# Start addresses of weight parts, h and activations in SBUF, and a shared buffer for the gates' linear

## The chip, the cores and the metric

The kernel runs on one core of a Trainium2 chip. The metric is the time of one execution on the device in microseconds (us), as the median of several runs. PE is TensorE, PEld its weight loads, DVE VectorE, ACT ScalarE, POOL GpSimd, SP the engine that issues the DMAs. A matmul here has two operands in SBUF. The **stationary** one (128 columns) is brought into the array by a weight load (LDWEIGHTS), the **moving** one (up to 512 columns) is streamed past it. The profile writes `bank<-w_hi,h_hi` for either order of the two.

## The reference

A block of three sublayer groups for one sequence of 256 tokens and width 1024, all in fp32:

```python
for i in range(2):                               # first_block
    shift, scale, gate = split(silu(c) @ ada_w[i] + ada_b[i], 3)
    h = rms_norm(x, norm_g[i]) * (1 + scale) + shift
    y = nsa_mixer(h, ...) if i == 0 else moba_mixer(h, ...)
    x = x + gate * y
x = x + 0.5 * swiglu(rms_norm(x), gate, up, down)      # second_block, hidden width 2816
proj = rms_norm(x) @ w_in                              # MLA and FoX attention, two gated branches
x = x + (sigmoid(g_mla + b) * (y_mla @ w_mla) + sigmoid(g_fox + b) * (y_fox @ w_fox)) @ w_o
x = x + 0.5 * swiglu(rms_norm(x), gate, up, down)
```

Each mixer is a set of linears around an attention over 256 tokens. In the first one the gates are `sigmoid(h @ w_gate + gate_b)` for three branches of 16 heads.

## The kernel before, in words

Activations are held with the width on the partitions: `h_hi` and `h_lo` are `[128, 8, 256]`, eight tiles of 128 features by 256 tokens. To keep fp32 precision with the fp32r matmul format, each number is split into a rounded part and its rest, and a product is three matmuls: hi·hi, hi·lo and lo·hi. The same is done with the outputs of attention (`o_hi`, `o_lo`, which lie in `qs` in the first block and in `o2_hi`, `o2_lo` in the second), the latents (`l_hi`, `l_lo`) and the hidden activations of the two feed-forward layers (`a1_hi`, `a1_lo`, `a2_hi`, `a2_lo`, 22 tiles each).

Weights come in **units** of 1024 columns (4 KB on each partition). SP fetches them one after another into seven buffers `w_raw0..6`. ACT rounds a unit into `w_hi[i % 4]` (`rounds`, L1105), DVE takes the rest into `w_lo[i % 4]` (`rests`, L1651), and PE uses them. A buffer of a part is free when PE's last matmul of the unit four earlier is done. The order of the units is one list (`unit_list`), and each engine's program is written out in that order.

Three places issue the large matmuls:

- `linear`, tokens out (L493): the stationary operand is a 128-token piece of `h`, `o` or `a`, the moving one 512 columns of a weight part (360 in `mix_lat`). A unit holds two tiles of the width, so for each unit and each half of the tokens it issues `w_hi, w_lo, w_hi, w_lo` against the hi activations and then `w_hi` twice against the lo ones.
- `linear`, features out (L505): the stationary operand is 128 columns of a weight part, the moving one 256 tokens of `h` or `o`, in the order (hi, hi), (hi, lo), (lo, hi).
- `tile_products` (L879): as L493, one half of the tokens at a time.

```python
xs = (hi, lo)[q][:, k0 + k + kk, t * P:(t + 1) * P]
mm = e.matmul(pb[t][:, 0:n], xs, (wh, wl)[p][:, kk * n:(kk + 1) * n],   # L493: stationary xs, moving w
mm = e.matmul(o, ws[p], xs[q], ...                                      # L505: stationary w, moving xs
```

SBUF is given out by `sb` in the order of the program, each buffer behind the one before it, with the start rounded up to 32 bytes. `mix`, `ffn1`, `mix2` and `ffn2` are four regions that begin at the same address, right behind `mask_r`, and are used in turn. `gate_lin` (1 KB, the last of the region `mix`) holds the gates' linear of the first block: DVE adds the bias into it (L2031), ACT takes the tanh in place (L1357), PE transposes it. `gated` (2 KB, in front of it) holds the gated outputs of attention of the first block (L1844).

Of the kernel before, what the change touches and what calls it, by code (L numbers as in the profile page):

```python
# [7 lines left out]
F32, F32R, I32 = mybir.dt.float32, mybir.dt.float32r, mybir.dt.int32  # L8
# [3 lines left out]
P = 128  # L12
D = 1024
S = 256
TT = S // P
KT = D // P
# [4 lines left out]
FT = FFN // P  # L21
# [11 lines left out]
UNIT = 1024  # L33
Z_FIRST = 5
NRAW, NSPLIT = 7, 4
# [154 lines left out]
def program(nc, wts, cols_d, rows_d, const_d, pos_d, gate_bias_d, x_d, out_d):  # L190
# [7 lines left out]
    ctx = ExitStack()  # L198
    with ctx:
        def sb(name, shape, dt=F32, on=ctx):  # L200
            return on.enter_context(nc.sbuf_tensor(name, shape, dt))
# [3 lines left out]
        def signal(name, by=1):  # L205
            signals.append(Signal(ctx.enter_context(nc.semaphore(name)), by))
            return signals[-1]

        raw = [sb(f"w_raw{i}", [P, UNIT]) for i in range(NRAW)]
        w_hi = [sb(f"w_hi{i}", [P, UNIT], F32R) for i in range(NSPLIT)]  # L210
        w_lo = [sb(f"w_lo{i}", [P, UNIT], F32R) for i in range(NSPLIT)]
        x = sb("x", [P, TT, D])
        h_hi, h_lo = (sb(n, [P, KT, S], F32R) for n in ("h_hi", "h_lo"))
        scr = sb("scr", [P, TT, D])
        cols, rows, const = sb("cols", [P, NCOLS]), sb("rows", [P, NROWS]), sb("const", [P, NCONST])
        pos = sb("pos", [P, NANG], I32)
# [14 lines left out]
                                   ("moba_k", ROT), ("mla_qr", MR))}  # L231
        ada_acc = [sb(f"ada_acc{i}", [P, 512]) for i in range(2)]
        unit_r, minus_r, mask_r = (sb(n, [P, P], F32R) for n in ("unit_r", "minus_r", "mask_r"))

        col = lambda n: cols[:, COLS[n][0]:COLS[n][1]]
        row = lambda n: rows[:, ROWS[n][0]:ROWS[n][1]]
# [18 lines left out]
        mix = ExitStack()  # L255
# [14 lines left out]
        parts_of_o = sb("parts_of_o", [P, TT, 2, 3, HD], on=mix)  # L270
        vc = sb("vc", [P, NKV, HD], on=mix)
        gated = sb("gated", [P, 2, S], on=mix)
        gate_lin = sb("gate_lin", [P, S], on=mix)
        pc_t = zs[:, 8:8 + NKV, :]
        z_tok = zs[:, 0:8, :].rearrange("p (t k) s -> p t (k s)", t=TT)

# [3 lines left out]
        ffn_a = {1: [sb(f"a1_{n}", [P, FT, S], F32R, on=ffn1) for n in ("hi", "lo")]}  # L280
# [15 lines left out]
        rs_row = sb("rs_row", [P, S], on=mix2)  # L296
        mix2.close()
        ffn2 = ExitStack()
        ffn_a[2] = [sb(f"a2_{n}", [P, FT, S], F32R, on=ffn2) for n in ("hi", "lo")]
        ffn_v[2] = [sb(f"act2_{n}", [P, TT, S], on=ffn2) for n in range(2)]  # L300
        ffn2.close()

# [2452 lines left out]
```

## Time and profile before

| | |
|---|---|
| runs, median of 3 | 917.91 us (917.71 to 919.36) |
| the profiled execution: span, first to last instruction | 916.3 us |
| runs less that span | 1.6 us |
| PE busy | 890.5 us, 97% |
| PEld busy | 760.4 us, 83% |
| DVE, ACT, POOL busy | 566.8, 494.0, 174.1 us |
| granted clock of PE | full, in all slices |
| DMA | 163.26 MB, mean 178 GB/s |

The profile shows no more than the span for the profiled execution, so its own time is taken as that span plus the 1.6 us. PE's busy time is the union of its matmuls; neighbouring matmuls overlap in it, since one that has begun to stream is not yet finished. What a matmul costs in a dense stretch is therefore not its duration but the step from its start to the next start.

### The profile page before, as it was taken

How to read it: one execution, taken by the hardware profiler on the slowest of the kernel's cores; microseconds unless marked ns; L12 is line 12 of the kernel's file. 1: busy time of each engine (PE TensorE's matmuls, PEld its weight loads, DVE VectorE, ACT ScalarE, POOL GpSimd, SP SyncE). 2: the span in 40 equal slices, each digit the busy share in tenths (PEclk: the TensorE clock that was granted, in tenths of full speed). 3: DMA queues.
4: the chain of work that ended last, by engine and by line, in shares of the span. 5: the costliest groups of instructions: out<-in, count | busy, mean ns of one | idle time of the engine just before them, and what ended most of it. 6: DMA issues, size and time to landing. Idle time of an engine off the chain costs nothing.

```text
span 916.3 us, 12879 instructions
## 1 busy us (share of the span) xinstructions
PE 890.5 (97%) x4925; PEld 760.4 (83%) x4925; DVE 566.8 (62%) x918; ACT 494.0 (54%) x780; POOL 174.1 (19%) x189
## 2 busy tenths in 40 slices
PE   3999999999999999999999999999999999999998
PEld 3789898998688988888888888798889888888886
DVE  5884787638878477555555556595557655555442
ACT  3634765555647646444444447676654654444431
POOL 1026265554065500000000004270000010000000
PEclk9999999999999999999999999999999999999999
DMA  9956665456473555555556555553344655555650
GB/s 360 375 170 207 208 214 177 127 150 198 141 259 94 183 184 161 184 185 185 184 185 206 156 151 181 161 162 92 94 118 152 189 186 185 187 185 187 212 168 24
DMA packets 45836, 163.26 MB, mean 178 GB/s; under 512 B 5200, under 2 KB 5584, under 8 KB 45776
## 3 DMA queue, kind: packets, MB, share of 16 engines
q1 hardware_dynamic: 45776, 162.44, 55.0%
q8 instruction: 40, 0.66, 0.3%
q14 instruction: 20, 0.16, 0.0%
HBM read 161.37 MB, written 1.05 MB: 177 GB/s over the span
## 4 chain that ended last, share of the span: by engine, by line
PE 86%; DVE 5%; ACT 4%; DMA 2%; issue 2%; POOL 1%; SPq 0%; DVEq 0%; ACTq 0%; POOLq 0%
PE bank L493 60%; PE bank L505 8%; PE bank L520 4%; PE bank L668 2%; PE bank L674 1%; PE bank L879 1%; DVE w_lo L1651 1%; DVE ada_acc L1733 1%; PE bank L695 1%; PE bank L696 1%; PE bank L694 1%; DMA x<-in_x 1%; PE bank L751 1%; DMA w_raw<-in_weights 1%; PE bank L600 1%
## 5 line engine op out<-in xcount | busy, mean ns | idle before, releaser
L1105 ACT ACTIVATE w_hi<-w_raw 128x1024 fp32r<-128x1024 f32 (+2 forms) x249 | 259.1, 1047 | 172.4 <-PE bank L493 153.7
L1651 DVE TENSOR_TENSOR w_lo<-w_raw,w_hi 128x1024 fp32r<-128x1024 f32 (+2 forms) x249 | 301.7, 1228 | 79.2 <-ACT w_hi L1105 78.6
L493 PE MATMUL bank<-w_hi,h_hi 128*128 128x512 f32 (+1 forms) x592 | 234.4, 396 | 0.8 <-issue 0.5
L493 PE MATMUL bank<-w_lo,h_hi 128*128 128x512 f32 (+1 forms) x592 | 229.8, 388 | 0.0
L493 PE MATMUL bank<-w_hi,h_lo 128*128 128x512 f32 (+1 forms) x592 | 181.9, 388 | 0.5 <-DVE h_lo L1680 0.5
L493 PEld LDWEIGHTS bank<-w_hi,h_hi 128*128 128x128 f32 x592 | 111.4, 188 | 23.3 <-issue 1.9
L493 PEld LDWEIGHTS bank<-w_hi,h_lo 128*128 128x128 f32 x592 | 110.9, 188 | 24.0 <-DVE h_lo L1680 0.9
L493 PEld LDWEIGHTS bank<-w_lo,h_hi 128*128 128x128 f32 x592 | 111.5, 188 | 21.0
L2486 POOL TENSOR_TENSOR ada_acc<-ada_acc,w_raw 128x512 f32<-128x512 f32 x56 | 79.3, 1417 | 78.3 <-ACT w_raw L1109 73.1
L493 PE MATMUL bank<-w_hi,a_hi 128*128 128x512 f32 x176 | 69.9, 397 | 0.0
L493 PE MATMUL bank<-w_lo,a_hi 128*128 128x512 f32 x176 | 69.7, 396 | 0.0
L2276 DVE SCALAR_TENSOR_TENSOR act<-bank,stats,act 128x256 f32<-128x256 f32 x44 | 21.1, 483 | 67.5 <-ACT act L1521 67.5
L505 PE MATMUL bank<-h_hi,w_hi 128*128 128x256 f32 x200 | 58.7, 293 | 0.2 <-ACT tok_k L1109 0.2
L505 PE MATMUL bank<-h_lo,w_hi 128*128 128x256 f32 x200 | 56.5, 283 | 0.0
L505 PE MATMUL bank<-h_hi,w_lo 128*128 128x256 f32 x200 | 56.5, 282 | 0.0
L493 PE MATMUL bank<-w_hi,a_lo 128*128 128x512 f32 x176 | 55.1, 394 | 0.0
L493 PEld LDWEIGHTS bank<-w_hi,a_lo 128*128 128x128 f32 x176 | 33.0, 188 | 8.1
L493 PEld LDWEIGHTS bank<-w_hi,a_hi 128*128 128x128 f32 x176 | 33.0, 188 | 7.9
L493 PEld LDWEIGHTS bank<-w_lo,a_hi 128*128 128x128 f32 x176 | 33.0, 188 | 7.8
L505 PEld LDWEIGHTS bank<-h_hi,w_hi 128*128 128x128 f32 x200 | 38.2, 191 | 1.2 <-issue 0.8
L2466 POOL TENSOR_TENSOR stats<-stats 128x2 f32<-128x2 f32 x4 | 7.0, 1753 | 168.4 <-DVE stats L1664 168.4
L505 PEld LDWEIGHTS bank<-h_lo,w_hi 128*128 128x128 f32 x200 | 38.2, 191 | 0.4 <-issue 0.2
(318 smaller groups left out, 1421.6 us busy)
## 6 DMA issues: line engine op xcount, KB each, us to landing
w_raw<-in_weights SPq DMA_DIRECT2D x298, 512.0 KB, 4.1
w_raw<-in_weights SPq DMA_DIRECT2D x4, 360.0 KB, 3.4
x<-in_x SPq DMA_DIRECT2D x1, 1024.0 KB, 9.3
gate_row<-in_gate_bias SPq DMA_DIRECT2D x2, 512.0 KB, 6.5
out<-x SPq DMA_DIRECT2D x4, 256.0 KB, 3.2
w_raw<-in_weights SPq DMA_DIRECT2D x3, 256.0 KB, 3.6
const<-in_constants SPq DMA_DIRECT2D x1, 285.5 KB, 5.4
cols<-in_columns SPq DMA_DIRECT2D x1, 208.5 KB, 2.5
```

Source lines behind the costliest of these rows:

```text
L493: mm = e.matmul(pb[t][:, 0:n], xs, (wh, wl)[p][:, kk * n:(kk + 1) * n], start=(k + kk == 0 and q == 0 and p == 0), stop=(k + kk == kts - 1 ...
L505: mm = e.matmul(o, ws[p], xs[q], start=(k + kk == 0 and i == 0 and b % 2 == 0), stop=(k + kk == kts - 1 and i == 2 and (b % 2 == 1 or b == ...
L520: mm = e.transpose(bank[0:int(np.prod(src.shape[1:])), o:o + src.shape[0]], src, ident)
L600: mm = e.matmul(bank[:, j * P:j * P + NB], r[:, kk * 256 + j * P:kk * 256 + (j + 1) * P], flat[i][:, k + kk, :], start=(k + kk == 0 and j ...
L668: e.matmul(o, k[:, g, br, j * P:(j + 1) * P], qs[:, ha:hb + 1:2, j * P:S], start=m == 0, stop=False, skip_group_check=True)
L674: mm = e.matmul(o[:, a, (t - j) * P:(t - j + 1) * P], bcast(mx[:, t, h, it["mx"]:it["mx"] + 1], [P, P]), minus_r[:, :], start=False, stop= ...
L694: e.matmul(o[0], p[:, a * S:a * S + P], v[0], start=True, stop=True)
L695: e.matmul(o[1], p[:, a * S + P:(a + 1) * S], v[0], start=True, stop=False)
L1105: e.activation(w_hi[i % NSPLIT][:, 0:c], raw[v % NRAW][:, 0:c], ACT.Copy).then_inc(*rounded(v))
L1651: e.tensor_tensor(w_lo[i % NSPLIT][:, 0:c], raw[v % NRAW][:, 0:c], w_hi[i % NSPLIT][:, 0:c].bitcast(F32), ALU.subtract).then_inc(*rested(v))
L2276: e.scalar_tensor_tensor(v, pairs[(p0 + n) % 2][tt][:, S:2 * S], norm_rs[i][:, tt:tt + 1], v, ALU.mult, ALU.mult).then_inc(*act_done((f, n ...
L2486: e.tensor_tensor(acc, acc, raw[u % NRAW][:, kk * 512:(kk + 1) * 512], ALU.add).then_inc(*ada_summed((c, k)))
```

## The change

The weights' parts, `h_lo` and the activations of the second feed-forward layer get gaps in front of them, and `gate_lin` becomes the first half of `gated`. On every engine the instructions are the same and stand in the same order; only the addresses differ, and the name of the tile in the four instructions on `gate_lin`.

```diff
@@ -206,11 +206,23 @@
             signals.append(Signal(ctx.enter_context(nc.semaphore(name)), by))
             return signals[-1]
 
+        gaps = []
+
+        def gap(n, on=ctx):
+            gaps.append(sb(f"gap{len(gaps)}", [P, n], on=on) if n else None)
+
+        def staggered(name, words):
+            for i, n in enumerate(words):
+                gap(n)
+                yield sb(f"{name}{i}", [P, UNIT], F32R)
+
         raw = [sb(f"w_raw{i}", [P, UNIT]) for i in range(NRAW)]
-        w_hi = [sb(f"w_hi{i}", [P, UNIT], F32R) for i in range(NSPLIT)]
-        w_lo = [sb(f"w_lo{i}", [P, UNIT], F32R) for i in range(NSPLIT)]
+        w_hi = list(staggered("w_hi", (0, 16, 16, 8)))
+        w_lo = list(staggered("w_lo", (8, 8, 8, 32)))
         x = sb("x", [P, TT, D])
-        h_hi, h_lo = (sb(n, [P, KT, S], F32R) for n in ("h_hi", "h_lo"))
+        h_hi = sb("h_hi", [P, KT, S], F32R)
+        gap(16)
+        h_lo = sb("h_lo", [P, KT, S], F32R)
         scr = sb("scr", [P, TT, D])
         cols, rows, const = sb("cols", [P, NCOLS]), sb("rows", [P, NROWS]), sb("const", [P, NCONST])
         pos = sb("pos", [P, NANG], I32)
@@ -231,6 +243,7 @@
                                    ("moba_k", ROT), ("mla_qr", MR))}
         ada_acc = [sb(f"ada_acc{i}", [P, 512]) for i in range(2)]
         unit_r, minus_r, mask_r = (sb(n, [P, P], F32R) for n in ("unit_r", "minus_r", "mask_r"))
+        gap(8)
 
         col = lambda n: cols[:, COLS[n][0]:COLS[n][1]]
         row = lambda n: rows[:, ROWS[n][0]:ROWS[n][1]]
@@ -270,7 +283,7 @@
         parts_of_o = sb("parts_of_o", [P, TT, 2, 3, HD], on=mix)
         vc = sb("vc", [P, NKV, HD], on=mix)
         gated = sb("gated", [P, 2, S], on=mix)
-        gate_lin = sb("gate_lin", [P, S], on=mix)
+        gate_lin = gated[:, 0, :]
         pc_t = zs[:, 8:8 + NKV, :]
         z_tok = zs[:, 0:8, :].rearrange("p (t k) s -> p t (k s)", t=TT)
 
@@ -296,7 +309,10 @@
         rs_row = sb("rs_row", [P, S], on=mix2)
         mix2.close()
         ffn2 = ExitStack()
-        ffn_a[2] = [sb(f"a2_{n}", [P, FT, S], F32R, on=ffn2) for n in ("hi", "lo")]
+        gap(32, ffn2)
+        ffn_a[2] = [sb("a2_hi", [P, FT, S], F32R, on=ffn2)]
+        gap(16, ffn2)
+        ffn_a[2].append(sb("a2_lo", [P, FT, S], F32R, on=ffn2))
         ffn_v[2] = [sb(f"act2_{n}", [P, TT, S], on=ffn2) for n in range(2)]
         ffn2.close()
```

Where the buffers begin, as the remainder of the start address by 512 bytes. Every piece of them that a large matmul reads begins at the same remainder as its buffer (the 360-column ones of `mix_lat` apart, whose second half begins 1440 bytes on):

```
buffer            before   after
w_raw0..6         128      128
w_hi0..3          128      128, 192, 256, 288
w_lo0..3          128      320, 352, 384, 0
x, h_hi           128      0
h_lo, scr         128      64
mask_r, unit_r    288      224
a1_hi, a1_lo      288      256
o2_*, l_*         288      256
qs, kh, kl        416      384
a2_hi             288      384
a2_lo             288      448
gate_lin          416      384 (gated)
```

The buffers of a large matmul where an operand's own start is a multiple of 32 but not of 64 are, before: all of `a`, `o2`, `l`, `qs`; after: `w_hi3` and `w_lo1`. The last buffer of the region `mix` ends 544 bytes lower than before.

## Rows read from the trace of the kernel before

**Rows 1.** The page: busy time of each engine, share of the span, instructions.

```profile
PE 890.5 (97%) x4925; PEld 760.4 (83%) x4925; DVE 566.8 (62%) x918; ACT 494.0 (54%) x780; POOL 174.1 (19%) x189
```

**Rows 2.** The page: the clock that PE was granted, in 40 slices.

```profile
PEclk9999999999999999999999999999999999999999
```

**Rows 3.** Windows: stretch; its length; busy us (instructions) of PE, PEld, DVE, ACT, POOL; clock.

```profile
29.50:150.00 120.50, 118.55 (x762) 105.47 (x762) 91.90 (x167) 67.46 (x106) 47.90 (x59) 1.00 0.66 227
...
350.00:480.00 130.00, 130.00 (x599) 107.58 (x598) 74.43 (x87) 66.08 (x87) 1.62 (x1) 1.00 0.58 186
...
843.00:916.30 73.30, 70.16 (x304) 56.33 (x302) 32.67 (x31) 25.10 (x26) 0.00 (x0) 1.00 0.43 136
```

**Rows 4.** The chain that ended last: start us, us, what, count of instructions.

```profile
125.37 3.81 DMA w_raw<-in_weights
...
143.12 2.87 PE bank L505 x24
...
250.33 27.20 PE bank L493 x120
...
334.26 11.19 PE bank L493 x48
...
480.46 33.60 PE bank L493 x144
...
542.98 3.98 PE bank L493 x24
...
684.12 2.81 PE bank L505 x24
...
854.37 58.81 PE bank L493 x252
```

**Rows 5.** Groups by line: busy us, mean ns, idle before with releaser.

```profile
L493 PE MATMUL bank<-w_hi,h_hi 128*128 128x512 f32 (+1 forms) x592 | 234.4, 396 | 0.8 <-issue 0.5 <-DVE tok_q L1715 0.2
...
L493 PE MATMUL bank<-w_hi,a_hi 128*128 128x512 f32 x176 | 69.9, 397 | 0.0
...
L505 PE MATMUL bank<-h_hi,w_hi 128*128 128x256 f32 x200 | 58.7, 293 | 0.2 <-ACT tok_k L1109 0.2
...
L493 PE MATMUL bank<-w_hi,qs 128*128 128x512 f32 x104 | 34.8, 402 | 1.2 <-DVE w_lo L1651 0.8 <-issue 0.4
...
L493 PE MATMUL bank<-w_lo,qs 128*128 128x512 f32 x52 | 20.6, 395 | 0.0
...
L505 PE MATMUL bank<-o_hi,w_hi 128*128 128x256 f32 x64 | 18.4, 287 | 0.0
...
L879 PE MATMUL bank<-w_hi,qs 128*128 128x512 f32 x24 | 7.7, 396 | 0.0
...
L879 PE MATMUL bank<-w_lo,qs 128*128 128x512 f32 x12 | 4.7, 396 | 0.0
```

**Rows 6.** Timelines, PE and PEld, at 854.44 us: start us, us, the instruction.

```profile
854.44 0.40 PE L493 MATMUL bank<-w_lo,a_hi 128*128 128x512 f32 x1
...
854.44 0.19 PEld L493 LDWEIGHTS bank<-w_hi,a_hi 128*128 128x128 f32 x1
```

**Rows 7.** Timeline, PE, from 542.9 us: matmuls of 360 columns.

```profile
542.98 0.33 PE L493 MATMUL bank<-w_lo,h_hi 128*128 128x360 f32 x1
543.14 0.33 PE L493 MATMUL bank<-w_hi,h_hi 128*128 128x360 f32 x1
543.31 0.33 PE L493 MATMUL bank<-w_lo,h_hi 128*128 128x360 f32 x1
```

**Rows 8.** Groups by line: the engines that make the weights' parts.

```profile
L1651 DVE TENSOR_TENSOR w_lo<-w_raw,w_hi 128x1024 fp32r<-128x1024 f32 (+2 forms) x249 | 301.7, 1228 | 79.2 <-ACT w_hi L1105 78.6
L1105 ACT ACTIVATE w_hi<-w_raw 128x1024 fp32r<-128x1024 f32 (+2 forms) x249 | 259.1, 1047 | 172.4 <-PE bank L493 153.7 <-DMA w_raw<-in_weights 15.4 <-PE bank L505 3.2
```

**Rows 9.** The tile gate_lin, then gated: duration min/median/max, first and last start.

```profile
L1357 ACT ACTIVATE gate_lin<-gate_lin x1: 422/422/422, 97.6 to 97.6; 128x256 f32<-128x256 f32 x1
...
L1844 DVE SCALAR_TENSOR_TENSOR gated<-bank,zs x4: 672/680/682, 175.1 to 221.6; 128x512 f32<-128x512 f32 x4
```

## The prediction

> **What bounds the kernel now.** I read the page's busy times first. PE is busy 97% of the span, no other engine over 62% [rows 1], and its clock is granted in full throughout [rows 2], which is the 2.4 GHz level. The windows tell where PE is the only limit: from 350 to 480 us it is busy for 130.00 of 130.00 us, and from 843 us on it lacks only the output's tail [rows 3]. From 29.5 to 150 us it is busy 118.55 of 120.50 us, but there the chain of waits also runs through other engines and transfers, for instance 3.81 us on a weight fetch [rows 4]. From 250 us on the chain is nearly one row of PE after another. So what counts is the **step** from one matmul's start to the next, and the chain's rows give it: us by count.
>
> The steps, from [rows 4], for a moving operand of 512 columns, which takes 512 / 2.4 = 213.3 ns at this clock:
>
> - stationary `h`, from 250.33 us: 27.20 / 120 = 226.7 ns, 13.4 over the columns;
> - stationary `qs`, from 334.26 us: 11.19 / 48 = 233.1 ns, 19.8 over;
> - stationary `a1`, from 480.46 us: 33.60 / 144 = 233.3 ns, 20.0 over; `a2`, from 854.37 us: 58.81 / 252 = 233.4 ns.
>
> For 256 moving columns (106.7 ns) they are 2.87 / 24 = 119.6 ns with `h` moving and 2.81 / 24 = 117.1 ns with `o2` moving, 12.9 and 10.4 over. The 360 columns of `mix_lat` (150.0 ns) step by 3.98 / 24 = 165.8 ns, 15.8 over.
>
> So one shape, 128 x 128 against 512 columns, costs 226.7 or 233.3 ns, by nothing that the program says except where the stationary operand lies. The next weight load starts with the matmul: a matmul with `w_lo` and the load for its successor, with `w_hi`, both start at 854.44 us [rows 6], so two reads of SBUF run together. The weights lie at remainder 128 of 512 bytes; `h` lies there too, `a` at 288 and `qs` at 416. The engines that make the weight parts are not the limit: ACT waited 153.7 us for PE to free a buffer, DVE 78.6 us for ACT [rows 8], and PE's idle time ahead of these matmuls is 0.8 and 1.2 us [rows 5].
>
> The Trainium skill speaks against any effect here. TensorE: Matmul & The Clock Gate, Step-by-step (Part 2), says that PE has two independent SBUF read ports, so that loading the next weights takes no bandwidth from the running matmul. SBUF — State Buffer, A bandwidth-pool intuition that's wrong, says that slowdowns come from a port lock and not from shared bandwidth. By these rules `h` and `a` would step alike; the 6.6 ns between them are not explained by them.
>
> **The change, part by part.** It adds and removes no instruction and moves none, so every engine's queue and every wait stays as it is.
>
> *1. The activations leave the odd remainders.* What parts the cheap from the dear steps in these rows can be read in two ways: by the distance between the two reads (0 for `h`, 160 for `a`, 288 for `qs`), or by whether the stationary operand begins at a multiple of 64 bytes (128 does; 288 and 416 don't). I take the second for this term: distances of 160 and 288 cost the same to 0.2 ns, which a position that mattered by itself would hardly do. After the change `a1`, `a2`, `l` and `qs` all begin at multiples of 64. The matmuls against `a` are 3 x 176 = 528, against `qs` 104 + 52 + 24 + 12 = 192 [rows 5]; together 720. Each falls from 233.4 to 226.7 ns: 720 x 6.7 = **4.8 us less**. Between the ends: nothing, or down to the 10.4 ns over the columns that `o2` shows, 720 x 9.6 = 6.9 us. Nearly all lie in stretches that are PE alone, so they count in full.
>
> *2. `o2` as moving operand.* It leaves 288, where it stepped 2.5 ns faster than `h`. There are 3 x 64 = 192 such matmuls [rows 5]: **0.5 us more**, if `h`'s price becomes its own.
>
> *3. The weights and `h` spread.* With `h_hi` at 0 and `h_lo` at 64, the weight parts at eight remainders, the distance 0 between a 512-column read and the next load is left only for `w_lo3`. By the reading of part 1 this does nothing for six of eight parts. `w_hi3` and `w_lo1` begin at 288 and 352, off 64 bytes. As moving operands they have a witness: the second half of each unit of `mix_lat` begins at remainder 32, and its step is 0.17 us against 0.16 us for the one in front [rows 7], no difference at this resolution. As stationary operands at L505 they are a quarter of 3 x 200 + 3 x 64 = 792; at worst 198 x 6.7 = 1.3 us more, at best nothing. I take **0**, since the short rows show no 6.7 ns anywhere. The whole of `h` at L493, 3 x 592 = 1776 matmuls, is the large unknown: one nanosecond on each is 1.8 us. Its ends are in the rivals.
>
> *4. ACT, DVE, DMA.* Their operands move too. Rounding takes 1047 ns and the rest 1228 ns a unit, 249 units each [rows 8], 259.1 and 301.7 us of 916.3. Even 10% more on both would stay hidden behind PE, for whom ACT waits 153.7 us; if that cover went, DVE's 78.6 us of waiting would be the next to go. **0**.
>
> *5. `gate_lin` in `gated`.* ACT's tanh is at 97.6 us, and `gated` is first written at 175.1 us [rows 9]. No wait is added. **0**.
>
> Sum: −4.8 + 0.5 = **−4.3 us**. The profiled execution has a span of 916.3 us, which becomes 912.0 us; the 1.6 us between span and the runs' median (917.9 us) put the forecast at **913.6 us**.
>
> **The rivals.**
>
> *A, it is the distance, and the chosen ones are good.* The loads' and the streams' reads meet in the same part of SBUF, and the spread keeps them apart. For it: `o2` at another distance costs 10.4 ns over the columns where `h` costs 12.9; all three distances seen at 512 columns cost more than that. If all large matmuls fell to 10.4 over: `h` at L493 1776 x 3.0 = 5.3 us, the 720 others 6.9 us, `h` at L505 600 x 2.5 = 1.5 us, in all 13.7 us less, **904.2 us**. Against it: no distance in the rows is near the bare columns, and the spread gives each pair another distance, so they can't all be the best.
>
> *B, nothing happens.* The 6.6 ns come from something that goes with the stage (the order over tiles, the banks), and addresses don't matter: **917.9 us**. This is what the skill's two pages above would give. Against it: `qs` and `a` come in stages with different orders and cost the same. That the change doesn't do what it says is out: the built program has the addresses.
>
> *C, slower: distance 0 was the cheap one.* Where both reads begin in the same place, the load follows the stream through SBUF and never crosses it; at every other distance they meet. For it: at 512 columns distance 0 is the cheapest of all rows, 226.7 against 233.1 and 233.4. The change takes `h` away from 0 in all but about 70 of its 1776 matmuls. If they step as `a` does now, that is 1700 x 6.7 = 11.4 us more, and `a` gains almost nothing, so **929 us** is its end; in the middle, half of that, **923.6 us**. It decides against the forecast from 4.3 us / 1776 = 2.4 ns on each `h` matmul. Against it: the 256-column rows, where 0 (119.6) is dearer than the other distance (117.1).
>
> **How the numbers follow.** The chances: forecast 0.35, A 0.26, B 0.12, C 0.27. A measurement of this kernel can tell about 0.2%, 1.8 us, from no change. The forecast and A are faster, B is the same, C is slower; a hundredth of the forecast's share goes to no change: 0.60, 0.13, 0.27. The likeliest single time is 913.6 us, its own range by the ends of parts 1 to 3 being 911.0 (6.9 less) to 914.9 (4.8 less, 0.5 and 1.3 more). The range for all cases runs from 902.0, a little below A, to 924.0, the middle of C; what lies above that is C's far end, and what lies below 902 would need steps that no row shows.
>
> **What would show it right or wrong.** In the changed kernel's chain the last PE row, 252 matmuls against `a2`, should fall from 58.81 to 57.1 us, the row of 144 against `a1` from 33.60 to 32.6 us, and the 48 against `qs` from 11.19 to 10.9 us, while the 120 against `h` stay at 27.20. If the `h` row falls as well, towards 26.8 us, A is right. If it rises to 27.6 us or more, C is. If no row moves, B. Unequal steps for the four buffers within one stretch, with `w_hi3` and `w_lo1` apart from the rest, would show that 64 bytes matter for the moving operand too.

## The result, and the profile after

The changed kernel takes 924.29 us (median of 6 runs, 923.33 to 927.26) against 917.95 us for the kernel before in the same set: a ratio of 1.0064, 95% interval 1.0051 to 1.0077. It is **slower by 6.3 us**.

The page of the changed kernel: its span, busy times as in [rows 1], and the granted clock.

```profile
span 925.5 us, 12879 instructions
...
PE 898.5 (97%) x4925; PEld 761.6 (82%) x4925; DVE 566.6 (61%) x918; ACT 494.0 (53%) x780; POOL 172.1 (19%) x189
...
PEclk9999999999999999999999999999999999999999
```

PE's instructions are the same 4925, and the busy times of the engines that feed it have not moved (DVE 566.8 to 566.6, ACT 494.0 to 494.0); POOL fell from 174.1 to 172.1 us. PE grew by 8.0 us, its weight loads by 1.2 us. The chain that ended last, with the rows that answer to those of [rows 4] (start us, us, what, count; line 493 is now 509, line 505 is 521):

```profile
146.97 2.88 PE bank L521 x24
...
254.15 27.85 PE bank L509 x120
...
338.95 11.12 PE bank L509 x48
...
487.55 33.38 PE bank L509 x144
...
698.35 11.48 PE bank L521 x96
...
852.58 11.15 PE bank L509 x48
864.17 58.17 PE bank L509 x252
```

By step: `h` as the stationary operand 27.85 / 120 = 232.1 ns, where it was 226.7; `qs` 11.12 / 48 = 231.7 (233.1 before); `a1` 33.38 / 144 = 231.8 (233.3); `a2` 58.17 / 252 = 230.8 (233.4). The last stretch of 48 against `h` takes 11.15 us, 11.00 before. At 256 moving columns nothing much changed (2.88 / 24 = 120.0 ns, 119.6 before). So the cheap steps and the dear ones have met near 231 ns, and `h` has by far the most matmuls. An estimate from the rows: 1776 x 5.4 = 9.6 us more on `h`; less on `a` (0.22 and 0.64 us in the two rows, 396 of its 528 matmuls, so 1.1 in all) and on `qs` (192 x 1.4 = 0.3 us). That is 8.2 us. Between the medians it is 6.3 us, so the estimate is too high, and its nearness to the 8.0 us more of busy time is in part chance, since the profiled execution is a long one. The term of `h` is the one that is too large. Summed from their starts in the trace of the kernel `weights_h_spread` below, which ran at the full clock throughout, the 1488 matmuls of 512 columns against `h` behind 250 us take 348.4 us, where they took 341.7 us before, and the 288 ahead of it, where PE also waits for other engines, 0.8 us more: some 7.5 us in all. The 600 matmuls of 256 columns with `h` give 0.7 us back.

The profiled execution has 3 us that the others lack: it is the run of 927.26 us, the other five lie between 923.33 and 924.48. Early on PE waited 1.75 us for `w_lo`, whose weights had come late (ACT had waited 6.94 us for that fetch, 5.37 us in the kernel before), and behind that wait it lost its clock for a while. The timeline of PE and two windows (stretch, length, busy us of PE, clock, DMA share, GB/s) of the changed kernel:

```profile
42.74 0.47 PE L509 MATMUL bank<-w_hi,h_hi 128*128 128x512 f32 x1 [1.75 <-DVE w_lo L1667]
```

```profile
40.00:45.00 5.00, 2.80 (x11) 0.91 0.98 389
45.00:50.00 5.00, 5.00 (x18) 0.75 0.87 311
```

From 45 to 50 us the granted clock averages 0.75, so PE was at its lower level, 1.2 GHz, for half of the time; it issues 18 matmuls, where 5 us hold 22 steps of 226.7 ns. The five other executions lack the 3 us, so this is not counted as a cost of the change. They have no trace; their mean granted clocks are 0.999 and 1.0, this one's 0.998.

### The profile page after: what moved, and what is told of

Its sections match the earlier page's. It is cut to its first block, busy times and chain, and to the rows that moved or that the text cites. A ratio compares the mean times of both kernels' runs of the same rounds, so it can differ in the third digit from the quotient of the medians.

```text
span 925.5 us, 12879 instructions
## 1 busy us (share of the span) xinstructions
PE 898.5 (97%) x4925; PEld 761.6 (82%) x4925; DVE 566.6 (61%) x918; ACT 494.0 (53%) x780; POOL 172.1 (19%) x189
## 4 chain that ended last, share of the span: by engine, by line
PE 87%; DVE 4%; ACT 4%; DMA 3%; issue 1%; POOL 1%; SPq 0%; DVEq 0%; ACTq 0%; POOLq 0%
PE bank L509 60%; PE bank L521 8%; PE bank L536 4%; PE bank L684 2%; DMA w_raw<-in_weights 2%; PE bank L690 1%; PE bank L895 1%; PE bank L711 1%; PE bank L712 1%; PE bank L710 1%; DMA x<-in_x 1%; DVE w_lo L1667 1%; PE bank L767 1%; ACT w_hi L1121 1%; PE bank L616 1%
## 5 line engine op out<-in xcount | busy, mean ns | idle before, releaser
L1121 ACT ACTIVATE w_hi<-w_raw 128x1024 fp32r<-128x1024 f32 (+2 forms) x249 | 259.2, 1047 | 177.3 <-PE bank L509 157.1
L1667 DVE TENSOR_TENSOR w_lo<-w_raw,w_hi 128x1024 fp32r<-128x1024 f32 (+2 forms) x249 | 301.8, 1229 | 81.8 <-ACT w_hi L1121 81.3
L509 PE MATMUL bank<-w_hi,h_hi 128*128 128x512 f32 (+1 forms) x592 | 237.5, 401 | 2.3 <-DVE w_lo L1667 1.7
L509 PE MATMUL bank<-w_lo,h_hi 128*128 128x512 f32 (+1 forms) x592 | 232.6, 393 | 0.0
L509 PE MATMUL bank<-w_hi,h_lo 128*128 128x512 f32 (+1 forms) x592 | 185.8, 395 | 0.5 <-DVE h_lo L1696 0.5
L2277 DVE SCALAR_TENSOR_TENSOR a_lo<-bank,a_hi 128x512 fp32r<-128x512 f32 x22 | 15.2, 692 | 37.9 <-ACT a_hi L1125 37.9
```

Of the source, the lines that this page charges most:

```text
L1121: e.activation(w_hi[i % NSPLIT][:, 0:c], raw[v % NRAW][:, 0:c], ACT.Copy).then_inc(*rounded(v))
L1667: e.tensor_tensor(w_lo[i % NSPLIT][:, 0:c], raw[v % NRAW][:, 0:c], w_hi[i % NSPLIT][:, 0:c].bitcast(F32), ALU.subtract).then_inc(*rested(v))
L2277: e.scalar_tensor_tensor(a_lo[:, 2 * n:2 * n + 2, :], b[:, :].rearrange("p (k t) -> p k t", k=2), 1.0, a_hi[:, 2 * n:2 * n + 2, :].bitcast ...
```

## The experiments

"Distance" is the start of the next stationary operand less the start of the running matmul's moving operand, modulo 512 bytes. All kernels compute the whole reference. In all of them `gate_lin` is the first half of `gated`, which pays for the gaps. A step is a chain row's time by its count, so a mean; "over" is that less 512 / 2.4 = 213.3 ns, which serves as the zero of the scale: no row here comes near it.

### All operands at one remainder

```diff
+        gap(88)                      # behind mask_r: the four regions begin at 128
-        qs = sb("qs", [P, NH, S], F32R, on=mix)
+        gap(96, mix)
+        qs = sb("qs", [P, NH, S], F32R, on=mix)
```

> The kernel before, with gate_lin in gated, and one gap ahead of the four regions and one ahead of qs, so that a, o2, l and qs begin at remainder 128 like the weights and h. Theory D (the step follows the distance between the moving operand and the next stationary one, 0 is cheapest): the 252 matmuls against a2 fall from 58.81 to 57.1 us, the 144 against a1 from 33.60 to 32.6, the 48 against qs from 11.19 to 10.9, h stays at 227; 913 us. Theory S (the stage sets it, not the address): nothing moves, 918 us. Theory 64 (multiples of 64 are cheap): as D here.

Measured: **914.38 us** against 918.40 us, ratio 0.9959 (0.9946 to 0.9971). It is faster than both kernels. The chain:

```profile
333.61 10.93 PE bank L500 x48
...
479.47 32.69 PE bank L500 x144
...
689.09 11.70 PE bank L512 x96
...
840.75 10.92 PE bank L500 x48
852.10 57.19 PE bank L500 x252
```

`qs` 227.7 ns, `a1` 227.0, `a2` 226.9: each fell from 233 to about what `h` costs, in the same stages with the same order and the same banks. The address alone does it. That part of the forecast's working (6.7 ns on each of 720 matmuls) has its size right, but not its reason: this kernel cannot tell a multiple of 64 from a distance of 0. The `o2` row (96 matmuls) went from 11.46 to 11.70 us, the size that part 2 gave for `o2` at the weights' remainder.

### Only the weights and h spread

```diff
-        w_hi = [sb(f"w_hi{i}", [P, UNIT], F32R) for i in range(NSPLIT)]
-        w_lo = [sb(f"w_lo{i}", [P, UNIT], F32R) for i in range(NSPLIT)]
+        w_hi = list(staggered("w_hi", (0, 16, 16, 8)))
+        w_lo = list(staggered("w_lo", (8, 8, 8, 32)))
...
         h_hi = sb("h_hi", [P, KT, S], F32R)
+        gap(16)
         h_lo = sb("h_lo", [P, KT, S], F32R)
+        gap(16)                      # all that follows begins as before
```

> Only the gaps of the weights' parts and of h as in the change, with a gap behind h_lo so that all that follows begins at the remainders of before. Theory D: h rises as in the change, from 227 to about 232 ns a matmul, and the activations (a against the spread weights) come near 232; 924 us. If the activations' move was what cost time in the change, this stays at 918 us.

Measured: **924.01 us**, ratio 1.0063 (1.0049 to 1.0076), the change's whole loss. The chain, `h` first, then `a2`:

```profile
250.29 27.85 PE bank L506 x120
...
860.29 58.47 PE bank L506 x252
```

`h` costs 232.1 ns as in the changed kernel. `a2`, which has not moved, costs 232.0, down from 233.4 by the weights' new places alone. So the activations' own moves, which the change makes besides, change nothing measurable on top of this: 924.01 us here (1.0063), 924.29 us with them (1.0064).

### Only the activations moved

```diff
+        gap(120)                     # behind mask_r: a1, o2, l at 256, qs at 384
...
+        gap(32, ffn2)                # a2_hi at 384
+        gap(16, ffn2)                # ahead of a2_lo: 448
```

> Only the activations' start as in the change (a1 256, a2 384 and 448, o2 and l 256, qs 384), weights and h at 128 as before. Theory 64: a and qs fall to 226.7 ns, 913 us. Theory D: a1 at distance 128, a2 at 256 and 320, qs at 256, each some 230 to 233 ns, since only 0 is cheap; 916 to 918 us.

Measured: **916.84 us**, ratio 0.9984 (0.9973 to 0.9995). The chain, `qs`, `a1`, `a2`:

```profile
333.37 10.93 PE bank L502 x48
...
479.41 33.60 PE bank L502 x144
...
853.30 58.28 PE bank L502 x252
```

`a1` begins at 256, a multiple of 64 like all operands here, and still costs 233.3 ns. That fells the reading on which the forecast stood. `qs`, at a distance of 256, costs 227.7 ns, as much as at 0 in `all_at_128`. This was foreseen by no theory and led to the scans. The small gain is `qs` and a part of `a2`, 58.28 us where it was 58.81. The two halves of the change do not add up: 1.6 us less here and 5.6 us more in `weights_h_spread` make 4.0 us more, and together they measured 6.3. The intervals, about 1 us either way each, leave room for a part of that.

### h moved to the distance that a has

```diff
+        gap(40)
         h_hi = sb("h_hi", [P, KT, S], F32R)
         h_lo = sb("h_lo", [P, KT, S], F32R)
+        gap(88)
```

> The kernel before, with h_hi and h_lo moved from remainder 128 to 288 and nothing else moved (gate_lin in gated pays for the gaps). Theory D: h gets the distance 160 that a has, so its 1776 matmuls step by 233.3 instead of 226.7 ns: 11 us more, 929 us, and 120 of them take 28.0 us instead of 27.20. Theory 64: the same, since 288 is off 64 bytes. Theory S: 918 us.

Measured: **927.70 us**, ratio 1.0098 (1.0085 to 1.0112), 9.3 us more. The chain:

```profile
251.82 28.00 PE bank L501 x120
...
852.35 11.20 PE bank L501 x48
```

28.00 us for 120, to the hundredth what was expected, 233.3 ns. `h` is only a stationary operand in these matmuls, so the address of what the weight loads read sets the step, together with the address of what streams. The whole is about 2 us less than the 11: the 256-column matmuls with `h` became a little cheaper (2.81 to 2.85 us for 24, from 2.87), and ahead of 250 us other engines share the chain.

### The scan of distances

Four kernels, one run each, with gaps that put `h`, `qs`, `a1` and `a2` at four different distances at a time; in the last, slices that begin four elements into a buffer eight elements longer.

```diff
+        gap(16)                      # scan_64, ahead of h_hi; 64 in scan_256, 120 in scan_480
+        gap(80)                      # scan_64, behind mask_r; 80 in scan_256, 48 in scan_480
+        gap(16, ffn2)                # scan_64, ahead of a2; 120 in scan_256, 8 in scan_480
...
+        def shifted(name, kt, on=ctx):     # scan_16
+            return sb(name, [P, kt * S + 8], F32R, on=on)[:, 4:4 + kt * S].rearrange("p (k s) -> p k s", k=kt)
```

> Weights all at 128; the distance from the moving weights to the next stationary operand is 64 for h, 160 for qs, 32 for a1, 96 for a2. Theory D (each distance has its own price): qs near 20 ns over the 213.3 of its columns, as a and h were at 160; h, a1 and a2 give new points, each above the 13.7 of distance 0. Theory D2 (price repeats every 256 bytes, since qs cost 15.2 at 256 as well as at 0): h at 64 then like 320. Theory M (what cost time in the change was that successive operands begin at different remainders, not the distance): all of them near 14.

> Distances 256 for h, 352 for qs, 224 for a1, 192 for a2, the same within each. Theory D2: h stays at 226.7 ns a step, since 256 is like 0. If h costs 20 over its columns here, the 15.2 of qs at 256 were its own. Theory M: all near 14.

> Distances 480 for h, 448 for qs, 320 for a1, 352 for a2. Theory D2: a2 at 352 like 96, h at 480 like 224, a1 at 320 like 64. Theory M: all near 14. A step under 13 ns over the columns would show a place better than 0, and give a layout faster than both kernels.

> Distances that are no multiple of 32: 16 for h, 96 for qs, 496 for a1, 48 for a2 (slices that begin four elements into their buffers). Theory D with fine structure: 16 and 496 differ from 0 and from each other; if a collision of the two reads is what costs, a shift by one line of 16 bytes either way should change the 13.7 ns, to under 10 or over 17. If only multiples of 32 bytes count, h stays at 13.7.

A fifth followed, with slices of two, six and four elements:

> Distances of 8 for h, -8 (504) for a1, -48 (464) for a2, the same within each. By the points so far (-16: 15.0, 0: 13.7, 16: 18.9, 32: 19.9; 192: 15.6, 224: 20.0): h between 13.7 and 18.9, a1 between 13.7 and 15.0, a2 between 15.6 and 20. Below 13.7 anywhere would give a layout better than all at one remainder.

The times were 927.03, 918.88, 928.16, 925.94 and 922.70 us, beside 918.59 us for the kernel before (918.34 for the last). The chains, in this order: `h`, `qs` (in `scan_480` alone; the row is 11.19 us in `scan_64` and 11.24 us in `scan_256`), `a1`, `a2`.

```profile
251.54 28.00 PE bank L503 x120
...
485.82 33.59 PE bank L503 x144
...
863.05 59.05 PE bank L503 x252
```

```profile
251.49 27.20 PE bank L503 x120
...
481.96 33.60 PE bank L503 x144
...
856.23 57.71 PE bank L503 x252
```

```profile
252.63 28.00 PE bank L503 x120
...
337.59 11.00 PE bank L503 x48
...
486.58 33.60 PE bank L503 x144
...
864.18 59.05 PE bank L503 x252
```

```profile
253.06 28.00 PE bank L509 x120
...
486.74 32.90 PE bank L509 x144
...
862.17 58.80 PE bank L509 x252
```

```profile
250.76 27.68 PE bank L509 x120
...
483.37 33.60 PE bank L509 x144
...
859.31 58.43 PE bank L509 x252
```

The step over 213.3 ns by distance modulo 256, the weights always at 128 and all operands of a kind at the same distance:

```
distance   over, ns   from
0          13.4       h before; 13.6 a2 and 14.4 qs in all_at_128; 256: 13.4 h in scan_256, 14.4 qs in activations_only
8          17.4       h in scan_8
16         20.0       h in scan_16
32         20.0       a1 in scan_64
48         20.0       a2 in scan_16
64         20.0       h in scan_64; 320: 20.0 a1 in scan_480
96         21.0       a2 in scan_64; 352: 21.0 a2 in scan_480
128        20.0       a1 in activations_only
160        20.0       h in h_at_288, a before
192        15.7       a2 in scan_256; 448: 15.9 qs in scan_480
208        18.6       a2 in scan_8 (464)
224        20.0       a1 in scan_256; 480: 20.0 h in scan_480
240        15.2       a1 in scan_16 (496)
248        20.0       a1 in scan_8 (504)
```

The price repeats every 256 bytes: five pairs agree to 0.2 ns, three of them with different operands and stages (64, 192, 224), and for 96 `qs` at 352 in `scan_256` (11.24 us for 48, 20.9 ns) is a third witness. There is a narrow cheap place at 0, two half-cheap ones at 192 and 240, and a plateau at 20 ns. Nothing is below 13.4. That `a` at 160 and `qs` at 288 cost the same was because both lie on the plateau. That it would cost by itself to go from one remainder to another, whatever the distance, which had all rows near 14 ns, is out: the weights here share one remainder. One expectation for `scan_8` missed: `a1` at 504 was to cost 13.7 to 15.0 ns and cost 20.0.

The table has a limit that no run here lifts. The weights begin at 128 in every row of it, so it can as well be read by the stationary operand's own start: cheap at 128 and 384, dear elsewhere. No kernel put all weight parts and an activation at one common remainder other than 128 or its partner 384. That the start of the moving operand counts too is shown by the next two kernels; that only the difference of the two counts is not shown.

### Only w_lo moved

```diff
-        w_lo = [sb(f"w_lo{i}", [P, UNIT], F32R) for i in range(NSPLIT)]
+        w_lo = list(staggered("w_lo", (16, 0, 0, 0)))      # (64, 0, 0, 0) in lo_at_384
+        gap(112)                                           # 64 in lo_at_384
         x = sb("x", [P, TT, D])
```

> The kernel before with only w_lo moved, from 128 to 192; h at 128. If each matmul pays for its own distance alone, two of the six against h pay 16 (distance 448, from the scan) and four pay 13.7: a mean of 14.4 ns over, no change in h to speak of. If it costs by itself that successive moving operands begin at different remainders (theory M), h rises well above, to 17 or more.

> The kernel before with only w_lo moved, from 128 to 384: all distances to h are 0 or 256. If the price repeats every 256 bytes, nothing changes at all, 918 us and h at 14. If the move from one remainder to another costs by itself, h rises.

Measured: 926.17 us and 917.73 us, beside 918.34 us. The chains, 120 and 48 against `h`:

```profile
251.79 27.93 PE bank L504 x120
...
850.82 11.17 PE bank L504 x48
```

```profile
842.53 11.00 PE bank L504 x48
```

With `w_lo` 256 bytes away nothing changes: 11.00 us, as before. With it 64 bytes away all of `h` costs 27.93 / 120 = 232.8 ns, though two of three moving operands are still at distance 0 and the third at a half-cheap one; paying each for its own distance would give 213.3 + (2 x 13.4 + 15.7) / 3 = 227.5. The timeline of PE in `lo_at_192` shows it matmul by matmul (start us, us, instruction):

```profile
253.49 0.40 PE L504 MATMUL bank<-w_hi,h_hi 128*128 128x512 f32 x1
253.73 0.39 PE L504 MATMUL bank<-w_lo,h_hi 128*128 128x512 f32 x1
253.96 0.63 PE L504 MATMUL bank<-w_hi,h_lo 128*128 128x512 f32 x2
```

The matmul at 253.49 us has `w_hi` moving and a piece of `h` next, a distance of 0, and the next starts 0.24 us behind it, not 0.227. Over the row, the matmuls with `w_hi` moving, all at distance 0, step by 228 to 241 ns, 233.0 in the mean; those with `w_lo` moving step by 232.5. In the kernel before they are all 226 or 227 ns. So the distance to the next stationary operand is not the whole rule. What the moving operands around it are counts as well: with one part out of step, the others lose the cheap place too.

### The best layout, with o2 apart

```diff
+        gap(8, mix2)                 # in all_at_128, ahead of o2_hi
+        gap(120, mix2)               # behind o2_lo
```

> all_at_128, and the outputs of attention of the second block (o2, which is only a moving operand, at L505) at 160 instead of 128. Where o2 moved at 160 and the weights stood at 128 its steps were 10.0 ns over their 106.7, against 13.0 in all_at_128: 192 matmuls x 3 = 0.6 us less, 913.8 us. Should the last row of 96 in the chain stay at 11.4 us, the scan's value for o2 does not carry over.

Measured: 914.45 us, ratio 0.9962 (0.9948 to 0.9975). The row of 96 with `o2` moving:

```profile
689.07 11.40 PE bank L514 x96
...
851.94 57.19 PE bank L502 x252
```

It fell from 11.70 to 11.40 us as expected. For all 192 such matmuls that is 0.6 us, which the medians (914.38 and 914.45) do not show. It is the same as all_at_128 within the measurement.

## Why the prediction was wrong

**What bounds the kernel** held: every time above follows PE's steps, and in the long rows of the chain nothing else came into it. Costing the change as steps times counts was a sound plan. What failed is the reading that set the steps, and with it two terms: 4.8 us of gain in part 1, and the 0 of part 3.

**Part 1 failed by its reason.** It said that `a` and `qs` were dear because they begin off a multiple of 64, and argued that 160 and 288 "cost the same to 0.2 ns, which a position that mattered by itself would hardly do". A plateau does just that: the scan shows 20 to 21 ns at nine of its fourteen distances. With `a1` moved to a multiple of 64 and the weights left alone it stayed at 233.3 ns. The term of 4.8 us measured 1.6 us in `activations_only`. In the changed kernel the rows of `a` and `qs` are 0.3 + 1.1 = 1.4 us shorter by the estimate above, but more than half of that on `a` comes from the weights' move: in `weights_h_spread`, where `a` lies as before, its two rows are 33.40 and 58.47 us, from 33.60 and 58.81.

**Part 3 is the term that decided.** "By the reading of part 1 this does nothing for six of eight parts", taken as 0, measured 5.6 us more for the whole kernel in `weights_h_spread`, with 5.4 ns on each `h` matmul in the long row (some 7.5 us on all of them, by the sums above). Weights and `h` had shared one remainder, and of all layouts tried only those in which the weights and the activation agree modulo 256 have the step of 226.7 ns. The working had the count and named it as the large unknown; the value was carried over from part 1 without a row of its own. The witness from `mix_lat`, 0.17 against 0.16 us, was too coarse: one step at a resolution of 10 ns can't tell 6.7 ns.

**Part 2** had its condition wrong for this change. With `o2` at the weights' remainder it is right in sign and size (11.46 to 11.70 us in `all_at_128`), but in the changed kernel the weights are spread, and the row went from 11.46 to 11.48 us: the 0.5 us did not come. **Parts 4 and 5** held: ACT and DVE kept 1047 ns and, in the changed kernel, 1229 ns a unit; `gate_lin` in `gated` costs nothing, since lo_at_384 has it and takes 917.73 us.

```profile
L1121 ACT ACTIVATE w_hi<-w_raw 128x1024 fp32r<-128x1024 f32 (+2 forms) x249 | 259.2, 1047 | 177.3 <-PE bank L509 157.1 <-DMA w_raw<-in_weights 16.9 <-PE bank L521 3.2
...
L1667 DVE TENSOR_TENSOR w_lo<-w_raw,w_hi 128x1024 fp32r<-128x1024 f32 (+2 forms) x249 | 301.8, 1229 | 81.8 <-ACT w_hi L1121 81.3
```

**Rival C** was what happened, by its own sign (`h` at 27.6 us or more; it took 27.85) and near the middle of its range: 923.6 us predicted for it, 924.3 measured, 0.3 us past the range's end. That the middle was so near is luck in part: it was set as half of the far end, 3.4 ns a matmul, and `h` rose by 5.4 ns in the long row, less in the early stages, with some given back by `a` and by the 256-column matmuls. Its evidence, that distance 0 was the cheapest of all 512-column rows, was the plain reading of [rows 4] and should have had more than 0.27. Its picture, a load that follows the stream and never crosses it, was not tested. It does not give the period of 256 by itself, nor the loss when `w_lo` alone is moved.

**Why the changed kernel's steps stop at 231 to 232 ns and not at 233.3 stays open.** One would say that a spread over many distances also meets the cheap ones at times, but its trace speaks against that. In its rows against `h`, `a1` and `a2`, 32 of the 144 places in the cycle of four buffers have a distance of 0 modulo 256. By the start times in the trace they step by 225 to 237 ns, 231.3 in the mean, and the 112 others by 231.6. (Which of the four buffers a matmul reads follows from the order in which ACT refills them.) The table holds only where all weight parts stand at one remainder, and both parts of the activation at one. Even there it gives means: at distance 160, `a1` before, the steps repeat as 238, 231, 231 ns, while at 0 none leaves 226 to 227.

**Rival A** was right that it hangs on where the two reads lie to each other, as far as these runs tell, and had the sign wrong: none of the fourteen distances tried is cheaper than 0 at 512 columns. At 256 columns there are cheaper ones: `o2` steps by 11.70 / 96 = 121.9 ns at distance 0 (`all_at_128`) and by 11.40 / 96 = 118.8 ns with its start at remainder 160, a distance of 480 (224 modulo 256), the row's start-up in both. But the 512-column matmuls carry the weight. **Rival B** is refuted: addresses matter. The Trainium skill, TensorE: Matmul & The Clock Gate, Step-by-step (Part 2), says that loading the next weights steals nothing from the running matmul because PE has two read ports. Here `h`, which in these rows only the weight loads read, moved by 160 bytes with the weights left where they were, and 120 matmuls went from 27.20 to 28.00 us. So the loads' address does change the pace of the matmuls; the measurement decides. What in SBUF or PE the two reads meet in stays open. So does which pairs of reads count: the next load against the running stream, one stream against the next, or both.

## What to carry to other kernels

Where PE is the bound with fp32r operands, take the step from start to start out of long chain rows, and compare it across operands: 3% of it depended on start addresses alone. Here all large operands at remainder 128 was best, a move by 256 bytes made no difference where it was tried (`h`, `qs`, `w_lo`), and staggering was what cost; one weight part out of step spoiled it for the rest. Whether another common remainder does as well was not measured. When two groups of rows differ and two readings explain them, price the change by the reading that needs no new assumption about the group that is already cheap, above all if that group has the most instructions.

## What the runs showed of the hardware that was not expected

- An fp32r matmul of 512 columns steps by 226.7 to 234.3 ns in the mean of a long row at the full clock, by where its operands begin modulo 256 bytes. With the weights at 128 the price changes within 8 bytes (distance 0: 13.4 ns over 213.3, 8: 17.4, 248: 20.0).
- The price is a property of the sequence, not of one matmul: `w_lo` moved by 64 bytes raised the mean of 120 in a row by 6.1 ns, and those at distance 0 stepped by 233.0 ns in the mean; moved by 256 bytes it changed nothing. In the changed kernel, with eight remainders of the weights, the distance of a single matmul says nothing about its step (231.3 ns at distance 0, 231.6 at the others).
- Where the weights and the activation share one remainder, all steps of a row are alike, 226 or 227 ns. With the activation elsewhere they differ in a short pattern that repeats, such as 238, 231, 231 ns at distance 160, though every matmul of the row has the same distance.
- A wait of 1.75 us by PE near 41 us was followed by a clock of 0.91 and 0.75 in the two stretches of 5 us around and behind it, in the one execution of six that was profiled, and that one took 3 us more.
